# Hybrid diffusion step on one core: merged operand by token tile, earlier ring releases, other order of block loads

## What is computed

```python
shift1, scale1, gate1, shift2, scale2, gate2 = split(silu(cond) @ w_ada + b_ada, 6)
h = rms_norm(x, norm1_g) * (1 + scale1) + shift1
z = h @ w_in                                  # pool channels | q | k | v | gate
pool_y = multiscale_pool(z[pool]) @ w_pool_out
ret_y = (silu(g) * group_norm(retention(q, k, v))) @ w_ret_out      # 4 heads, two directions
gates = sigmoid(h @ w_branch_gate + b_branch_gate)
merged = gates[:D] * pool_y + gates[D:] * ret_y
x = x + gate1 * (merged @ w_out)
h2 = rms_norm(x, norm2_g) * (1 + scale2) + shift2
# expert choice: 16 SwiGLU experts of width 2816, each takes its top 64 latent and 16 context tokens
x = x + gate2 * moe(h2, w_router, w_gate, w_up, w_down)
y = rms_norm(x, final_norm_g)
```

## Time and profile before

| | before |
|---|---|
| median of 3 runs | 2005.39 us (2004.25 to 2009.44) |
| the profiled execution | 2004.61 us, its span 2002.8 us |
| PE busy | 1956.9 us, 98% of the span |
| DVE, ACT, POOL busy | 455.3, 239.2, 277.8 us |
| DMA | 649.51 MB, mean 324 GB/s |
| chain that ended last | PE 91%, DMA 5% |

### The profile page before, as it was taken

The page is one execution under the profiler, slowest core; times in us unless marked ns, Lnnn a source line. Parts: engine busy times, 40 slices in busy tenths (PEclk is TensorE's granted clock), DMA queues, the critical chain, the costliest instruction groups (busy, mean ns, idle before and its releaser), DMA issues.

```text
span 2002.8 us, 53587 instructions
## 1 busy us (share of the span) xinstructions
PE 1956.9 (98%) x24626; PEld 1204.7 (60%) x24626; DVE 455.3 (23%) x892; ACT 239.2 (12%) x426; POOL 277.8 (14%) x316
## 2 busy tenths in 40 slices
PE   8999999999988999999999999999999999999996
PEld 6888899999873444554444544445544445544443
DVE  3532441232644111111111121111111111021113
ACT  4332333122320000000000000000000000000001
POOL 3032019000411010101101011010101101011020
PEclk9999999999988999999999999999999999999999
DMA  9244542312249999999999999999999999999996
GB/s 342 83 158 143 174 128 63 106 61 80 84 187 370 417 410 418 408 419 408 415 415 408 419 408 418 411 409 418 409 419 408 411 419 409 419 409 413 417 404 257
DMA packets 149500, 649.51 MB, mean 324 GB/s; under 512 B 9980, under 2 KB 54904, under 8 KB 133064
## 3 DMA queue, kind: packets, MB, share of 16 engines
q1 hardware_dynamic: 134576, 617.71, 76.7%
q0 software_dynamic: 14688, 30.98, 5.3%
q10 hardware_dynamic: 184, 0.06, 0.0%
HBM read 633.45 MB, written 15.38 MB: 324 GB/s over the span
## 4 chain that ended last, share of the span: by engine, by line
PE 91%; DMA 5%; DVE 1%; issue 1%; POOL 1%; ACT 0%; SPq 0%; POOLq 0%; DVEq 0%; ACTq 0%
PE bank L2036 43%; PE bank L2109 21%; PE bank L1711 17%; PE bank L1832 3%; PE bank L1979 2%; DMA a_raw<-in_w_ada_dram 1%; DMA y_tile<-acc_scratch 1%; DMA ring<-in_w_exp_down_dram 1%; PE bank L1693 1%; PE bank L1682 1%; DMA acc_scratch<-out_rows,idx_scatter 1%; DMA h_scratch<-h 1%; PE bank L2148 0%; PE bank L1928 0%; PE bank L1916 0%
## 5 line engine op out<-in xcount | busy, mean ns | idle before, releaser
L2036 PE MATMUL bank<-ring,xs_t 128*32 128x352 f32 x12288 | 920.5, 461 | 7.4 <-DMA ring<-in_w_exp_up_dram 5.7
L2036 PEld LDWEIGHTS bank<-ring,xs_t 128*32 128x32 f32 x12288 | 399.5, 110 | 516.4 <-issue 500.3
L2109 PE MATMUL bank<-ring,hid_t 128*32 128x256 f32 x8184 | 447.3, 379 | 0.0
L2109 PEld LDWEIGHTS bank<-ring,hid_t 128*32 128x32 f32 x8184 | 266.0, 110 | 180.6 <-issue 10.3
L1569 DVE TENSOR_TENSOR hid<-silu_g,bank 128x352 f32<-128x352 f32 x96 | 44.2, 516 | 767.2 <-PE bank L2036 767.2
L1088 ACT ACTIVATE silu_g<-bank 128x352 f32<-128x352 f32 x96 | 37.6, 464 | 1298.6 <-PE bank L2036 1298.6
L743 POOL TENSOR_TENSOR small<-kpow 128x2 f32<-128x2 f32 x31 | 14.2, 459 | 1166.3 <-DVE out_rows L1599 1140.5
L1575 DVE STREAM_TRANSPOSE hid_t<-hid 128x352 f32<-128x352 f32 x93 | 69.3, 796 | 354.7 <-PE bank L2109 354.7
L1711 PE MATMUL bank<-act_hi,wt_hi 128*128 128x320 f32 x448 | 138.8, 310 | 0.8 <-DVE rtmp L1380 0.8
L1711 PE MATMUL bank<-act_hi,wt_lo 128*128 128x320 f32 x448 | 138.4, 309 | 0.0
L1711 PE MATMUL bank<-act_lo,wt_hi 128*128 128x320 f32 x448 | 138.4, 309 | 0.0
(11 more groups left out here) (306 smaller groups left out, 1555.0 us busy)
## 6 DMA issues: line engine op xcount, KB each, us to landing
ring<-in_w_exp_gate_dram SPq DMA_DIRECT2D x128, 1408.0 KB, 27.9
ring<-in_w_exp_up_dram SPq DMA_DIRECT2D x128, 1408.0 KB, 24.4
ring<-in_w_exp_down_dram SPq DMA_DIRECT2D x96, 1536.0 KB, 25.9
ring<-in_w_exp_down_dram SPq DMA_DIRECT2D x32, 1024.0 KB, 26.8
raw_t<-in_w_ada_dram SPq DMA_DIRECT2D x16, 1024.0 KB, 5.4
raw_t<-in_w_in_dram SPq DMA_DIRECT2D x14, 1024.0 KB, 6.5
a_raw<-in_w_ada_dram SPq DMA_DIRECT2D x8, 1024.0 KB, 16.0
raw_t<-in_w_branch_gate_dram SPq DMA_DIRECT2D x8, 1024.0 KB, 5.7
```

Of the source, the lines that this page charges most:

```text
L2036: ins = mm(bank[UP_BANK[x] if up else x][c * Q:(c + 1) * Q, 0:FC], xs_t[:, x, k * Q:(k + 1) * Q], w[:, kk, c * FC:(c + 1) * FC], start=k = ...
L2109: ins = mm(bank[6 + x // 2][c * Q:(c + 1) * Q, x % 2 * DC:(x % 2 + 1) * DC], hid_t[:, f, x * Q:(x + 1) * Q], w[:, j, c * DC:(c + 1) * DC], ...
```

## The change

The merged operand is now one tile, `merged`, laid out by token tile (for each of five positions its high and low parts for all channels), where it was two tiles over all tokens. The two spans of `po` are 384 and 256 tokens wide, where both were 320. `ORDER` becomes 4, 3, 0, 1, 2. Two of the `wo` operands move, and the ring's slots are renumbered so that slot 0 lies over `sig_p` and slots 1 and 2 over the first positions of `merged`. PE releases slot 0 in the last block of tile `ORDER[0]`, slots 1 and 2 with the first matmul of `wo_chunk(3, 0)`, and 5 slots in `router(3)`. In the block list the first `ada` block now stands ahead of `("v", 2)`. The split of `("v", 2)` moves on ACT and DVE to the head of head 0, where two splits now follow one another.

```diff
--- before.py
+++ after.py
@@ -38,7 +38,9 @@
 SPLIT_T = 2
 PIECES = 8
 WHOLE = 12
-ORDER = (4, 0, 1, 2, 3)
+ORDER = (4, 3, 0, 1, 2)
+PO_SPAN = ((0, 384), (384, 640))
+PO_POS = ((2, 5), (0, 2))
 QK_ORDER = ((0, 1, 2, 3), (2, 3, 0, 1))
 WARM = (10, 6, 5, 3)
 
@@ -104,7 +106,7 @@
 def trunk_blocks():
 
     ada = [("ada", b) for b in range(8, 24)]
-    heads = [("v", 0), ("v", 1), ("v", 2)] + ada[:2] + [("v", 3)] + ada[2:12] + [("g", 0)] + ada[12:] + [("g", 1)]
+    heads = [("v", 0), ("v", 1), ada[0], ("v", 2), ada[1], ("v", 3)] + ada[2:12] + [("g", 0)] + ada[12:] + [("g", 1)]
     return ([("a1", i) for i in range(PIECES)] + [("qk", i) for i in range(4)] + heads
             + [("g", 2), ("g", 3)] + [("u", 0), ("u", 1)] + [("sr", b) for b in range(4)]
             + [("ro", b) for b in range(4)] + [("sp", b) for b in range(4)] + [("po", 0), ("po", 1)]
@@ -242,6 +244,7 @@
 
         A, X, CC, RT, HT, M0 = 0, 45056, 65536, 116736, 141312, 174080
         act_hi, act_lo = at("act_hi", A, [P, KT, T], F32R), at("act_lo", A + 20480, [P, KT, T], F32R)
+        merged = at("merged", A, [P, NT, 2, KT, P], F32R)
         cos_t, sin_t = at("cos_t", A + 40960, [P, NS, DK]), at("sin_t", A + 43008, [P, NS, DK])
         x_in = at("x_in", X, [P, NT, D])
         o_t = at("o_t", X, [P, KT, T])
@@ -316,13 +319,14 @@
         pool_a = at("pool_a", dead, [P, 2, 544])
         gtmp = at("gtmp", dead + 4352, [P, 2, HALF])
         rtmp = at("rtmp", dead + 6912, [P, 2, HALF])
+        po_tmp = at("po_tmp", dead + 4352, [P, 2, 384])
         g1_b = at("g1_b", dead + 9472, [P, 2, D])
         gs2_b = at("gs2_b", dead + 17664, [P, 2, D])
         adar = at("adar", dead + 25856, [96, P])
         assert dead + 25856 + 512 <= 229344 - base
 
         ring = [at(f"ring{i}", o, [P, PIECE]) for i, o in enumerate(
-            (0, 12288, 24576, 61440, 73728, 86016, 98304, 147456, 159744, 110592, 122880, 135168))]
+            (98304, 0, 12288, 24576, 61440, 73728, 86016, 147456, 159744, 110592, 122880, 135168))]
 
 
         def wt(b, wide, extra, out):
@@ -337,9 +341,9 @@
 
             return wt(b, wt_lo, wv_lo, wo_lo)
 
-        wo_hi = [wt_hi[:, 1, :], wt_hi[:, 0, :], at("wo_hi2", CC, [P, WB], F32R)[:], at("wo_hi3", CC + 40960, [P, WB], F32R)[:]]
+        wo_hi = [wt_hi[:, 1, :], wt_hi[:, 0, :], at("wo_hi2", CC, [P, WB], F32R)[:], at("wo_hi3", CC + 24576, [P, WB], F32R)[:]]
         wo_lo = [wt_lo[:, 1, :], wt_lo[:, 0, :], at("wo_lo2", CC + 8192, [P, WB], F32R)[:],
-                 at("wo_lo3", CC + 24576, [P, WB], F32R)[:]]
+                 at("wo_lo3", CC + 16384, [P, WB], F32R)[:]]
         r_tmp = [at("r_tmp0", CC + 49152, [P, 512]), at("r_tmp1", dead + 4096, [P, 512])]
         x2_sq = at("x2_sq", RT, [P, D])
         h2_t = at("h2_t", RT + 8192, [P, 2, D])
@@ -698,8 +702,9 @@
             for y in range(24, 40):
                 ct, f = divmod(y - 24, 2)
                 pool.wait_ge(s_ghi, y + 1)
-                nc.gpsimd.tensor_tensor(act_lo[:, ct, f * HALF:(f + 1) * HALF], rtmp[:, y % 2, :],
-                                        act_hi[:, ct, f * HALF:(f + 1) * HALF].bitcast(F32), ALU.subtract).then_inc(s_glo, 1)
+                n, ps = PO_SPAN[f][1] - PO_SPAN[f][0], slice(*PO_POS[f])
+                nc.gpsimd.tensor_tensor(merged[:, ps, 1, ct, :], po_tmp[:, y % 2, 0:n].rearrange("p (t q) -> p t q", q=P),
+                                        merged[:, ps, 0, ct, :].bitcast(F32), ALU.subtract).then_inc(s_glo, 1)
 
             for d in (h2_dram, acc_dram):
                 pool.dma_start(d[L_P:SPARE_END, :], x_prompt[0, 0:Q - C_P, :]).then_inc(s_spare, 16)
@@ -971,11 +976,11 @@
             for lt in range(2, NT):
                 v_out(0, lt)
                 qk_t("k", lt, tr)
-                if lt < 4:
+                if lt == 2:
                     split_next()
 
             for h in range(H):
-                if h in (0, H - 1):
+                for _ in range((2, 0, 0, 1)[h]):
                     split_next()
                 for kind, i, *u in head_steps(h):
                     if kind == "v":
@@ -1036,7 +1041,10 @@
                             ct = 4 * i + cc
                             z = 2 * ct + f
                             act.wait_ge(s_gmul, 24 + z + 1)
-                            nc.scalar.activation(act_hi[:, ct, span], rtmp[:, z % 2, :], ACT.Copy).then_inc(s_ghi, 1)
+                            n = PO_SPAN[f][1] - PO_SPAN[f][0]
+                            nc.scalar.activation(merged[:, slice(*PO_POS[f]), 0, ct, :],
+                                                 po_tmp[:, z % 2, 0:n].rearrange("p (t q) -> p t q", q=P), ACT.Copy)\
+                              .then_inc(s_ghi, 1)
             for i in range(1, 4):
                 split(NTH["wo", i])
 
@@ -1298,7 +1306,6 @@
                 if lt == 2:
                     decay_tables()
             split_next()
-            split_next()
             dve.wait_ge(s_tab, 11)
 
             def decayed_scores(h):
@@ -1408,16 +1415,18 @@
                               .then_inc(acc_read["dve"], 1)
                         elif kind == "po":
                             ct = 4 * i + cc
-                            src = acc((kind, i, cc, f))[:, 0:HALF]
+                            span = slice(*PO_SPAN[f])
+                            n = span.stop - span.start
+                            src = acc((kind, i, cc, f))[:, 0:n]
                             if z >= 2:
                                 dve.wait_ge(s_glo, z - 1)
                             dve.wait_ge(acc_read["act"], ACT_READ_SP)
                             if ct == 0 and f == 0:
                                 dve.wait_ge(acc_read["dve"], DVE_READ_RO)
-                            nc.vector.tensor_tensor(rtmp[:, z % 2, :], src, sig_p[:, ct, span], ALU.mult)\
+                            nc.vector.tensor_tensor(po_tmp[:, z % 2, 0:n], src, sig_p[:, ct, span], ALU.mult)\
                               .then_inc(acc_read["dve"], 1)
                             dve.wait_ge(acc_read["dve"], DVE_READ[kind, i, cc, f])
-                            nc.vector.tensor_tensor(rtmp[:, z % 2, :], rtmp[:, z % 2, :], mix[:, ct, span], ALU.add)\
+                            nc.vector.tensor_tensor(po_tmp[:, z % 2, 0:n], po_tmp[:, z % 2, 0:n], mix[:, ct, span], ALU.add)\
                               .then_inc(s_gmul, 1)
                             z += 1
             dve.wait_ge(s_glo, z)
@@ -1732,8 +1741,8 @@
                 for cc in range(width // P):
                     cs = slice(cc * P, (cc + 1) * P)
                     for f in range(2):
-                        o = acc(b + (cc, f))[:, 0:HALF]
-                        fs = slice(f * HALF, (f + 1) * HALF)
+                        fs = slice(*PO_SPAN[f]) if b[0] == "po" else slice(f * HALF, (f + 1) * HALF)
+                        o = acc(b + (cc, f))[:, 0:fs.stop - fs.start]
                         pairs = [pr for k in range(kts) for pr in (
                             (wh[:, k, cs], hi[:, k, fs]), (wh[:, k, cs], lo[:, k, fs]), (wl[:, k, cs], hi[:, k, fs]))]
                         three(o, pairs, 3 * kts).then_inc(acc_full, 1)
@@ -1973,8 +1982,7 @@
             def wo_mm(i, j, c, kk, z):
 
                 k = 2 * j + kk
-                sl = slice(ORDER[i] * P, (ORDER[i] + 1) * P)
-                a = (act_hi, act_lo, act_hi)[z][:, k, sl]
+                a = merged[:, (ORDER[i] + 2) % NT, (0, 1, 0)[z], k, :]
                 w = (wo_hi, wo_hi, wo_lo)[z][j][:, kk * D + c * 512:kk * D + (c + 1) * 512]
                 return mm(bank[WO_BANKS[i % 3][c]][:, :], a, w, start=k == 0 and z == 0, stop=k == KT - 1 and z == 2)
 
@@ -1984,6 +1992,8 @@
                     for kk in range(2):
                         for z in range(3):
                             ins = wo_mm(i, j, c, kk, z)
+                            if i == 3 and c == 0 and j + kk + z == 0:
+                                ins.then_inc(e_used, 2)
                 ins.then_inc(wo_full, 1)
 
             def h2_transpose(i):
@@ -2004,7 +2014,7 @@
                     ins = mm(bank[LG_BANK[lt]][:, lt * NE:(lt + 1) * NE], h2_t[:, i % 2, k * P:(k + 1) * P], wr_sb[:, k, :],
                              start=k == 0, stop=k == KT - 1)
                     if i == 3 and k == 0:
-                        ins.then_inc(e_used, EARLY)
+                        ins.then_inc(e_used, EARLY - 3)
                 ins.then_inc(s_lg, 1)
 
             def aff_transpose(group, tiles):
@@ -2050,6 +2060,8 @@
                                 ins = wo_mm(i, j, c, kk, z)
                                 if j == 3 and kk == 1 and z == 2:
                                     ins.then_inc(wo_full, 1)
+                                elif j == 3 and kk == 1 and z + i + c == 0:
+                                    ins.then_inc(e_used, 1)
             pe.wait_ge(s_const, 16 * N_CONST)
             wo_banks(2)
             wo_chunk(2, 0)
```

## The result

The changed kernel takes 2012.03 us, median of 11 runs (2010.35 to 2014.81). The kernel before, run beside it, takes 2005.39 us (2003.88 to 2009.44, 11 runs). The ratio is 1.0031, 95% interval 1.0022 to 1.004, which is 4.4 to 8.0 us: slower, by about what a measurement can tell. The forecast of 2013.8 us was 1.8 us too high. The profiled execution has a span of 2009.6 us, 6.8 us more than before.

What follows compares the result with a forecast made beforehand. It took PE to bound trunk and experts, and a serial DVE, PE and POOL chain the hand-over. 3.8 + 1.7 + 1.7 + 1.7 - 0.5 = +8.4 us gave 2013.8 us, own range 2012 to 2015, wider range 2005.5 to 2017.5.

Steps and rivals of the forecast that it cites:

- Sign, place and mechanism: Slower: in head 0 value block 3 lands late, ACT stands at its split, and PE waits for ACT's modulation copy.
- PE's wait is 129.8 - 125.99 = +3.8: Head 0: PE waits for ACT's copy for the first modulation block's columns, +3.8 us, bounds 3.8 to 8.5.
- The work lost is 1.7 us. A wait of 3.8 us should do no less: Behind the head-0 wait: PE's clock falls, +1.7 us, bounds 0 and 1.7.
- 6 x 0.29 = 1.7: Merge: the wide span lengthens each of six rounds by 0.29 us, +1.7 us, bounds 0 and 3.4.
- PE would then wait 1.2 + 1.7 = 2.9 us at that place: Before the second `wo` block: the longer wait makes PE's clock fall, another +1.7 us, bounds 0 and 1.7.
- -0.5: Hand-over: earlier slot releases remove PE's wait for the sixth weight piece before the spread, -0.5 us.
- the gather as a place where up to 1 us could go: Hand-over: POOL's gather could gain from a quieter queue; nothing taken, -1 us kept as that end.
- rival 2: The head-0 wait does not come or is absorbed, merge alone costs 1.2 to 2.9 us: 2006.6 to 2008.3 us, chance 0.10.
- rival 4: Faster: expert weights set the hand-over, so all 7.1 us of PE's weight waits go: 1998.3 us, chance 0.08.
- Rival 1: The waits come but the clock does not fall at one or both places: 2010.4 to 2012.1 us, chance 0.17.

Runs made afterwards that it cites:

- e1: The changed kernel with the block list and split places of the kernel before: 2006.20 us, ratio 1.000 to the kernel before.
- e2: The kernel before with only the changed block list and split places: 2013.32 us, ratio 1.0036.
- e3: The changed kernel with ACT's split of value block 3 moved behind the first two modulation copies of head 0: 2005.93 us, ratio 0.9998.
- e8: The kernel before with the new split places as its only edit: 2011.21 us, ratio 1.003.
- e7: The kernel before with the new block list order as its only edit: 2013.32 us, ratio 1.0046.
- e10: The changed kernel with the first gate block one modulation block later in the list: 2008.42 us, ratio 1.0013.
- e11: e10 with 16 small unused matmuls ahead of PE's wait in head 0: 2006.53 us, ratio 0.9999 to the kernel before.
- e5: e1 with all 8 ring slots released in `router(3)` again, so no early releases: 2006.01 us, ratio 1.0004 to the kernel before.
- e9: e1 with the first gate block one modulation block later in the list: 2002.74 us, ratio 0.9984 to the kernel before.
- e12: e9 with unused small matmuls (12, 2 and 4) around the hand-over's last transposes and router: 1998.70 us, ratio 0.9968 to the kernel before.
- e6: The kernel before with merge spans of 384 and 256 as its only edit, old layout kept: 2005.58 us, ratio 0.9999.
- e4: The changed kernel with 16 small unused matmuls ahead of PE's wait for the first modulation copy: 2013.15 us, ratio 1.0037 to the kernel before.

## Why the prediction was right, and where not

**Sign, place and mechanism** were right. The step "PE's wait is 129.8 - 125.99 = +3.8" was measured as 3.9 us, its parts within 0.3 us: issue 121.99 and 121.89, end of the copy 129.8 and 129.75. e1, e2 and e3 show that this, and not the landing, is the cause. That it depends on list and split places was not in my working: I had it from the list alone, and e8 shows that the splits do it as well.

**"The work lost is 1.7 us. A wait of 3.8 us should do no less"** was undersized by one half. I took the price of a 2.3 us wait for one of 3.8 and wrote it as the upper bound too. The loss is 3.4 us in all four profiles in which that wait was 3.8 us or more and stood open (the change, e2, e7, e10). In time it is about 3 us: 6.9 - 3.9 in the change, and 2.9 between e11 and e10 by the load of the first `ro` block.

**"6 x 0.29 = 1.7" for the merge** was the wrong step: PE's wait grew by 0.3 us. A round grew by 0.09 us and not by 0.29, and only the three rounds behind the second split show in the wait. Of the members, DVE's multiplication (0.07) was right and ACT's copy (0.04) a little small at 0.06. DVE's addition was not: I had 0.07 for it, and it did not grow. POOL's was not: I added 0.11 us for 64 columns, as if all its units were alike, and the one on the round became 0.05 us shorter. The mean of 983 ns before hides two durations, as the pair shown above has them: the first unit takes 1.08 to 1.09 us, the second 0.87 to 0.88. The slope between 256 and 384 columns is (1033 - 736) / 128 = 2.3 ns a column, not my 1.66, and 736 + 64 x 2.3 = 884 is the faster kind. The Trainium skill, GPSIMD Engine Reference, section 3.1, has 2.6 cycles an element, at 1.2 GHz an estimate of 2.2 ns: for the slope the Trainium skill was nearer than the row that I took, which is of the pooling additions. What slows the first unit of each pair of before may be DVE. POOL's pair starts at 522.40 while DVE's addition of 522.26 runs for another 0.35 us, and in the change the overlap is 0.15 us (523.90 against 523.62 + 0.43). The Trainium skill, GPSIMD Engine Reference, section 1, says that POOL shares its way to SBUF with VectorE and contends with instructions that have two SBUF inputs, as this addition has. No run here takes the overlap away alone, so this is argued and not shown.

**"PE would then wait 1.2 + 1.7 = 2.9 us at that place", and so another +1.7**, fell with the step before it: the wait was 1.5 us, and no profile shows a loss there.

**"-0.5" for the releases**: 0.5 up to the spread, by the profiles and by e5. A further 0.3 us lies behind it. In the earlier trace rows the experts start 5.12 us after the gather's start (619.46 to 624.58), and now 4.84 (626.03 to 630.87): DVE's last transposition is 0.65 us, since the first half of the rows was turned while the second was under way. I had named the gather as a place where up to 1 us could go and taken nothing.

**Sum.** By the profiles: 6.8 at the first `ro` block (3.9 of wait and about 3 of clock, less 0.1), 0.2 for the merge, -0.8 for the hand-over, and 0.5 behind the start of the experts, for which the forecast had no term: 6.8 us, the span's difference, with the parts rounded. The forecast had 8.4. The clock in head 0 was over 1 us too small, and the merge with its clock had 3.4 where 0.2 was. So it was luck in part that the total came closer than its parts, and that 2012.03 lies just inside my own range of 2012 to 2015. Of rival 2 (no wait in head 0) and rival 4 (weights set the hand-over) nothing is left. Rival 1 holds at one of its two places: no fall at the merge.

## What to carry to other kernels

When loads share a few slots, a reordered list changes, for each load, whose use frees its slot; write down that event for every moved load, and then what stands behind the engine that waits for it. Here a late block cost nothing until its consumer stood at it with finished work behind; moving that one wait behind two copies was worth 6 us. Removing a stall pays only up to the next wait of the same kind, so look for that one first: of 3.0 us gained in head 0, all went at the next late block until its load was moved too. And one profile of each kernel is not enough to place a difference of 2 us in the whole: follow the same few instructions through both, from the first difference to the end, as the tails of e9 and e12 show.

## What was not expected of the hardware

**The clock's losses come in steps.** In every trunk stretch of the profiles they add up to 1.7 or 3.4 us, never between. The length of the wait alone does not give the price. A wait of 1.2 to 1.5 us before the second `wo` block cost nothing in any profile. A wait of 2.2 to 2.3 in head 3 cost 1.7 in seven, and nothing in e6. One of 2.5 in e8 cost 3.4. And behind a wait of 0.4 us for ACT's `h_t`, near 573 us, the clock fell in e5 and e11 and in no other:

```profile
574.58 0.27 PE L1692 MATMUL bank<-ident,aff 128*16 128x128 f32 x1 [0.40 <-ACT h_t L1065]
```

```profile
573.00:576.00 3.00, 2.60 (x15) 2.09 (x15) 0.02 (x1) 2.16 (x4) 0.00 (x0) 0.80 0.00 0
576.00:579.00 3.00, 3.00 (x10) 2.36 (x9) 1.09 (x3) 1.77 (x4) 0.00 (x0) 0.63 0.02 5
```

That is 3 x (0.20 + 0.37) = 1.7 us in e5. For a forecast, a wait in this trunk is worth its length plus a loss of 0, 1.7 or 3.4 us (the last was about 3 us of time), and one profile can be off by such a step. The tail scatters more: in 1962 to 1989 us the loss lies between 1.7 and 8.6 us in the fourteen profiles.

**Small filler matmuls hold the clock**: 16 of them in a gap of 3.9 us (e4, e11), and 18 around the router (e12), kept it at 1.00 through the stretch that they filled.
